# In the recurrence, VectorE's order within a half product: step first, then the next weight unit's split and the conditioning block's sum

## The reference, cut to what matters

```python
h = _rmsnorm(x, p['norm1_w'][l]) * (1 + sc1) + sh1        # sc, sh, g: conditioning, silu(c) @ ada_w
proj = jnp.einsum('bld,de->ble', h, p['w_in'][l])         # (L, 1024) x (1024, 4096)
q, ff, fb, iv, g, hy = jnp.split(proj, cuts, axis=-1)
...
o_f, s_f = _chunk_scan(qh, k_f, vh, logf_f, s0[:, 0])     # S_t = diag(f_t) S_{t-1} + k_t v_t^T
o_b, s_b = _chunk_scan(rev(qh), rev(k_b), rev(vh), rev(logf_b), s0[:, 1])
o = o_f + rev(o_b)                                        # then a norm per head and a gate silu(g)
...
z = _long_conv(u, kern) + p['hy_d'][l].astype(F32) * u    # the Hyena half of the channels
out = jnp.einsum('ble,ed->bld', merged, p['w_out'][l])    # then residual, norm 2 and the ConvFFN
```

## Time and profile before

| | |
|---|---|
| three runs | 965.82, 971.62, 971.90 us; median 971.62 |
| profiled execution | 968.83 us, span 967.0 us |
| TensorE (PE) busy | 932.1 us, 96% of the span |
| PE weight loads | 830.5 us, 86% |
| VectorE (DVE) busy | 620.3 us, 64% |
| ScalarE (ACT) busy | 339.3 us, 35% |
| chain that ended last | PE 79%, DVE 14%, ACT 3%, issue 2%, DMA 1% |
| mean granted TensorE clock | 0.989 of full |

### The profile page before, as it was taken

The page is one execution under the profiler, slowest core; times in us unless marked ns, Lnnn a source line. Parts: engine busy times, 40 slices in busy tenths (PEclk is TensorE's granted clock), DMA queues, the critical chain, the costliest instruction groups (busy, mean ns, idle before and its releaser), DMA issues.

```text
span 967.0 us, 13859 instructions
## 1 busy us (share of the span) xinstructions
PE 932.1 (96%) x5630; PEld 830.5 (86%) x5630; DVE 620.3 (64%) x809; ACT 339.3 (35%) x599; POOL 24.3 (3%) x34
## 2 busy tenths in 40 slices
PE   8988999999999999999999999999999999999996
PEld 4457889898898899687789899889999988999985
DVE  4844565884966976699586666445666644566655
ACT  2734243424333324233463433211333321233332
POOL 1100000100000000002000000000000000000000
PEclk9998999999999999999999999999999999999999
DMA  9746142343143334408121221222222221222102
GB/s 308 244 138 208 44 153 88 94 142 127 45 151 137 109 138 142 124 8 197 65 87 46 91 83 67 87 88 66 67 87 66 75 100 66 66 71 82 44 1 109
DMA packets 34407, 99.37 MB, mean 103 GB/s; under 512 B 3767, under 2 KB 11959, under 8 KB 33576
## 3 DMA queue, kind: packets, MB, share of 16 engines
q1 hardware_dynamic: 30760, 86.10, 26.8%
q0 software_dynamic: 3264, 12.35, 4.7%
q10 hardware_dynamic: 320, 0.04, 0.0%
HBM read 95.31 MB, written 3.16 MB: 102 GB/s over the span
## 4 chain that ended last, share of the span: by engine, by line
PE 79%; DVE 14%; ACT 3%; issue 2%; DMA 1%; ACTq 0%; DVEq 0%; SPq 0%
PE ps L1504 22%; PE ps L1505 22%; PE ps L1506 22%; PE ps L1731 3%; PE ps L1524 2%; DVE w_lo L1020 1%; PE ps L1743 1%; PE ps L1594 1%; PE ps L1868 1%; DMA hcol<-in_vec 1%; ACT w_hi L695 1%; PE ps L1751 1%; DMA raw<-in_slots 1%; PE ps L1532 0%; ACT xn L927 0%
## 5 line engine op out<-in xcount | busy, mean ns | idle before, releaser
L1504 PE MATMUL ps<-h_hi,w_hi 128*128 128x320 f32 x1152 | 362.6, 315 | 9.6 <-DVE w_lo L1020 5.4
L1505 PE MATMUL ps<-h_lo,w_hi 128*128 128x320 f32 x1152 | 357.6, 310 | 0.0
L1506 PE MATMUL ps<-h_hi,w_lo 128*128 128x320 f32 x1152 | 357.5, 310 | 0.0
L1504 PEld LDWEIGHTS ps<-h_hi,w_hi 128*128 128x128 f32 x1152 | 218.1, 189 | 11.2 <-ACT w_hi L695 4.4
L1505 PEld LDWEIGHTS ps<-h_lo,w_hi 128*128 128x128 f32 x1152 | 218.1, 189 | 0.1
L1506 PEld LDWEIGHTS ps<-h_hi,w_lo 128*128 128x128 f32 x1152 | 217.8, 189 | 0.0
L1020 DVE TENSOR_TENSOR w_lo<-raw,w_hi 128x1024 fp32r<-128x1024 f32 x106 | 129.4, 1225 | 112.7 <-ACT w_hi L695 109.1
L695 ACT ACTIVATE w_hi<-raw 128x1024 fp32r<-128x1024 f32 x106 | 110.8, 1052 | 94.1 <-PE ps L1506 91.6
L1505 PE MATMUL ps<-w_lo,a_hi 128*128 128x512 f32 x220 | 85.6, 389 | 0.0
L1504 PE MATMUL ps<-w_hi,a_hi 128*128 128x512 f32 x220 | 85.6, 389 | 0.0
L1506 PE MATMUL ps<-w_hi,a_lo 128*128 128x512 f32 x220 | 85.6, 389 | 0.0
(11 more groups left out here) (267 smaller groups left out, 1041.3 us busy)
## 6 DMA issues: line engine op xcount, KB each, us to landing
raw<-in_slots SPq DMA_DIRECT2D x138, 512.0 KB, 3.7
raw<-in_slots SPq DMA_DIRECT2D x24, 256.0 KB, 6.7
xin<-in_x_sample SPq DMA_DIRECT2D x4, 512.0 KB, 10.4
grow<-gates POOLq DMA_DIRECT2D x2, 1024.0 KB, 13.2
x<-in_x_sample POOLq DMA_DIRECT2D x2, 1024.0 KB, 13.4
out_y_sample<-x SPq DMA_DIRECT2D x4, 512.0 KB, 3.1
decay<-in_decay POOLq DMA_DIRECT2D x1, 1280.0 KB, 10.4
ktab<-in_ktab POOLq DMA_DIRECT2D x1, 1024.0 KB, 12.3
```

The source lines that it names most:

```text
L1504: mm(out, lhs[0], rhs[0], start=first, stop=False)
L1505: mm(out, lhs[0], rhs[1], start=False, stop=False)
L1506: return mm(out, lhs[1], rhs[0], start=False, stop=last)
```

## The change

In the halves from n = 6 on, `split_lo` is done behind `step` instead of ahead of it, and `sum_groups` is behind `step` in all halves. `pass_k` and `bound_gates` stay ahead. No instruction is added or taken away, and the other engines' programs are the same.

```diff
                 if step_at(n):
                     pass_k(*step_at(n))
-                for unit in ahead(n):
-                    split_lo(unit)
+                if n < 2 * HEAD_TILES:
+                    for unit in ahead(n):
+                        split_lo(unit)
+                if n % 2 and kind in ("ff", "fb"):
+                    eng.wait_ge(sem("half_free"), n + 1)
+                    bound_gates(i, int(kind == "fb"))
+                if step_at(n):
+                    step(*step_at(n))
+                if n >= 2 * HEAD_TILES:
+                    for unit in ahead(n):
+                        split_lo(unit)
                 if n in ADA_SUM:
                     e = ADA_SUM[n]
                     sum_groups(e)
                     if ADA_ORDER[e] == FINE[1]:
                         make_gain(1, "norm2")
-                if n % 2 and kind in ("ff", "fb"):
-                    eng.wait_ge(sem("half_free"), n + 1)
-                    bound_gates(i, int(kind == "fb"))
-                if step_at(n):
-                    step(*step_at(n))
                 if n % 2 and kind == "fb":
                     start_head(i)
```

## The result

The changed kernel takes 980.03 us (median of 4 runs, 975.92 to 982.18) against 970.19 us before (4 runs, 965.82 to 971.90): a ratio of 1.0113, 95% interval 1.0079 to 1.0147. The profiled execution takes 980.09 us with a span of 978.3 us, 11.3 us more than before. The same kernel timed again later gave 1.0114 (1.0086 to 1.0142).

A forecast was written before the change was run, and what follows sets the result against it. TensorE, busy 96% of the span, was taken as the bound, with VectorE pacing only halves 14 to 19. Profiled 968.8 + 8.7 (turns) + 5.1 (clock) = 982.6, plus half of 2.8: 984 us; 8-in-10 range 968 to 990, own 979 to 989.

The forecast's parts named there:

- The split of halves 18, 30 and 42: On VectorE, the split moves behind QQ, small product and copy, 3.28 us later in head 1, delaying the slot's load.
- The turns: TensorE's turns wait for the late loads: +3.3, +2.1 and +3.3 us in heads 1 to 3, together +8.7 us.
- Head 1's reason: In head 1 the late split's load was last ahead of the turn, so the turn goes from 204.73 to 208.0.
- The clock: TensorE's clock halves behind the longer turn waits, losing 1.7 us in each of three heads, +5.1 us.
- The rule drawn from the earlier trace: TensorE waits of 2.14 and 2.24 us were followed by half clock; waits of 1.1 us and less were not.
- NORM halves: Halves 14, 26, 38, 50: split moves behind finish_head, costing 1.14 us there; slots freed 11 us later cost nothing.
- the rival of late pieces: Slots freed late at the NORM halves also delay half 18's products, some 3 us a head: 992 us; chance 0.10.
- Level 0: Halves 16, 28, 40: QQ starts 0.42 us earlier (0.6 in head 2); TensorE's 2.9 us of waits shrink by some 1.5.
- all there is to win: TensorE's waits in three heads of the recurrence, 2.9 us ahead of a level and 0.6 ahead of a turn.
- Head 0: Half 6: the later split's load still reaches the turn in time, at 137.4 before 138.20; no cost, 0.8 us cover.
- Not slower: The ring is not on the path to the turn, so only the gain is left: 965 to 969 us; chance 0.15.
- Full clock: The turns wait as forecast but TensorE stays at full clock: 977.5, or about 979 us; chance 0.20.

The follow-up runs named there:

- after_swap: Changed kernel, but ScalarE does ada_row ahead of split_hi in the halves with a turn; 0.9969 of the kernel before.
- turn_only: Kernel before, with only the splits of halves 6, 18, 30 and 42 moved behind the step; 1.0068 of the kernel before.
- sum_only: Kernel before, with only the sum moved behind the step and all splits left ahead of it; 1.0013 of the kernel before.
- after_busy: Changed kernel plus ten unused 128-column matmuls on TensorE ahead of the turn in halves 20, 32 and 44; 1.0117 of the kernel before.
- norm_only: Kernel before, with only the splits of halves 14, 26, 38 and 50 moved behind finish_head; 1.0043 of the kernel before.
- after_busy2: Changed kernel plus 15, 11 and 15 unused matmuls in the turn waits of heads 1, 2 and 3; 1.0093 of the kernel before.
- after_swap_norm: Changed kernel with ada_row ahead of split_hi and the splits of halves 14, 26, 38 and 50 ahead of the step; 0.9949 of the kernel before, 963.02 us.
- after_stream: Changed kernel, but the weight unit stands behind the first of four conditioning pieces in the load stream; 1.0058 of the kernel before.
- but_turn: Changed kernel, but in halves 6, 18, 30 and 42 the split stays ahead of the step; 1.0072 of the kernel before.
- stream_gates: after_stream with GpSimd's stores of the gates moved from ahead of the first state's store to behind the second's; 0.9992 of the kernel before.

## Why the prediction was right, step by step

- **The split of halves 18, 30 and 42, +3.28 us.** Measured 3.27 (head 1) from the reciprocal. That it reaches the turn through the ring is shown from both sides: with the turn ahead of `split_hi` the loss is gone (after_swap), and moving these splits alone costs 0.7% (turn_only).
- **The turns, +8.7 us.** Measured +7.7: 2.4, 2.3 and 3.0 against 3.3, 2.1 and 3.3. The loads took 4.25, 3.27 and 4.25 us instead of the 5.1, 3.2 and 4.5 taken over; the term was 1.0 us too large. The prediction's estimate of 3.2 us for a load, from the Trainium skill (DMA: Bandwidth & Descriptors, Anatomy of one DMA), uses a fit that the section gives for transfers issued by GpSimd; these are SyncE's, and only head 2's load (3.27 us) took that time.
- **Head 1's reason was half of it.** The prediction priced the moved sum as a gain of 0.4 us and looked past GpSimd, which waits for `mod_ready` of that block. In every profile in which the stores stood ahead of it but one, head 1's load landed 15 to 17 us behind their start, whether it was issued at 193.4 or at 201.3 (turn_only, with early stores and a late issue, 18.8). In the changed kernel both the late slot and the late stores end there, so either alone delays head 1 (turn_only +1.9, sum_only +2.5) and they do not add.
- **The clock, +5.1 us.** Measured +4.7 by turn to reciprocal; in the profiled execution all three turns had it. By the mean clocks above, about half of the ten executions of the changed kernel had fewer stretches of half clock; if those behind the turns are among the missing, the term is smaller in them, and that it came out whole in the profile is in part luck. The size per fall held (1.5 to 1.7 us). The rule drawn from the earlier trace rows was too strong: of waits of about 1.9 to 2.5 us in the recurrence, one in after_busy and one of three in norm_only were followed by a fall, and neither of the two in turn_only (2.54 and 2.36 us). The Trainium skill (TensorE: Matmul & The Clock Gate, Part 1) says that the half rate is the default and activity lifts it; these rows agree, and after_busy2, with the engine kept active, has no fall.
- **NORM halves.** Cost at the head of the stretch 1.14 us, priced well; alone they cost 0.4% (norm_only). The slots freed 11 us later hurt nobody, as priced, so the rival of late pieces did not occur.
- **Level 0, a gain of 1.5 us at most.** The waits fell by 1.0 us (2.9 to 1.9). That 3.5 us are "all there is to win" was too low: in after_swap_norm the time from the first reciprocal to the last is 193.25 us, 4.7 us less than before.
- **Head 0.** No wait at its turn, as priced: w_hi waited 1.81 us for the load, inside the cover.
- **The rivals.** Not slower: its deciding point, a split at 196.7 or earlier, was missed by 2 us, 3.3 from the reciprocal. Full clock: no. In the sum 13.8 us were forecast against the 12.46 of the recurrence. The rest of the distance from 984 to 980.03 is the base: half of 2.8 us was added for a median of 971.6 that is 970.19 with a fourth run, and this execution's first 100 us were 1.2 us shorter.

## What to carry to other kernels

An instruction that frees a buffer has two customers: whoever uses its result, and whoever refills the buffer. Moving it behind a waiting step is paid by the second one, and the place to look is the first in-order engine behind the refill: here one copy on ScalarE stood behind a load that it did not need. Cut that tie first; then the reordering that cost 1.1% gave, together with the cut, 0.3%, and 0.5% with the four splits that had been in idle time put back.

## What the runs showed of the hardware

- Small stores held up large loads long after their issue. Two stores of `gates` (4 KB each, in elements of 4 bytes that lie apart) and one state store (128 KB) were issued over 2.5 us by GpSimd; a 512 KB load issued at the end of them took 13.18 us (after_stream), one issued 6 us later 7.6 to 8.2 us (sum_only, but_turn), and the same load without them 3.6 us (stream_gates). Behind a state store alone loads took 3.8 to 5.4 us, among the gates' stores up to 13.3 us (stream_gates). Why 8 KB do this is not shown.
- The granted clock does not follow the length of TensorE's wait alone: 2.54 us left it full in turn_only, in after_busy 1.87 us behind added work was followed by a fall and 1.78 us was not, and all six waits of 2.5 us and more in the two profiles of the changed kernel were.
